# Trainium2, one core: the scan's output with tokens as rows, a fourth weight buffer, and feed-forward loops of four steps

## What is computed

```python
def step(state, inp):                      # one chunk of 32 tokens, one head, one direction
    qc, kc, vc, gc = inp
    bcum = jnp.cumsum(gc, axis=2)
    qe, ke = qc * jnp.exp(bcum), kc * jnp.exp(-bcum)
    att = jnp.where(causal_in_chunk, jnp.einsum('bhtk,bhsk->bhts', qe, ke), 0.0)
    o = jnp.einsum('bhtk,bhkv->bhtv', qe, state) + jnp.einsum('bhts,bhsv->bhtv', att, vc)
    ...
def _hg_readout(o, g, norm_w):             # o is the sum over both directions
    o = o * lax.rsqrt(jnp.mean(o * o, axis=-1, keepdims=True) + EPS)
    return o * norm_w * silu(g)
def conv_ffn_2(h, w_up, conv_w, conv_b, w_down):
    a, val = jnp.split(h @ w_up, 2, axis=-1)
    return (gelu(dwconv3(a, conv_w, conv_b)) * val) @ w_down
```

## Time and profile before

| | |
|---|---|
| median of 3 runs | 1513.62 us (1512.83 to 1514.57) |
| profiled execution, its own time | 1513.27 us |
| its span, first to last instruction | 1511.5 us |
| PE busy | 97% of the span, 10486 matmuls and as many weight loads |
| DVE busy | 72% |
| ACT busy | 48% |
| HBM read | 181 GB/s over the span |
| mean granted TensorE clock | 0.989 |

### The profile page before, as it was taken

The page is one execution under the profiler, slowest core; times in us unless marked ns, Lnnn a source line. Parts: engine busy times, 40 slices in busy tenths (PEclk is TensorE's granted clock), DMA queues, the critical chain, the costliest instruction groups (busy, mean ns, idle before and its releaser), DMA issues.

```text
span 1511.5 us, 26784 instructions
## 1 busy us (share of the span) xinstructions
PE 1461.0 (97%) x10486; PEld 1298.9 (86%) x10486; DVE 1082.4 (72%) x1659; ACT 732.3 (48%) x949; POOL 6.8 (0%) x19
## 2 busy tenths in 40 slices
PE   7989999999999999999999999899999999999997
PEld 7887889999987889999888779679999899799997
DVE  6774778778756787777766666667777768677775
ACT  6553545444545555445555433545444433454442
POOL 0000000000000000000000000000000000000000
PEclk9999999999999999999999999999999999999999
DMA  7433645555556344554526566055455554555551
GB/s 279 154 140 130 259 167 189 197 177 189 190 200 259 132 176 169 194 192 168 215 85 223 199 248 237 20 199 199 172 190 182 203 201 167 185 200 174 192 180 43
DMA packets 39677, 274.79 MB, mean 182 GB/s; under 512 B 4528, under 2 KB 5680, under 8 KB 6960
## 3 DMA queue, kind: packets, MB, share of 16 engines
q1 hardware_dynamic: 38304, 265.82, 48.9%
q0 software_dynamic: 720, 6.82, 1.2%
q10 hardware_dynamic: 576, 1.05, 0.2%
HBM read 272.62 MB, written 1.05 MB: 181 GB/s over the span
## 4 chain that ended last, share of the span: by engine, by line
PE 86%; DVE 7%; DMA 3%; ACT 3%; issue 2%; SPq 0%; DVEq 0%; ACTq 0%
PE L L1750 25%; PE D L1750 16%; PE L L1938 15%; PE L L1944 8%; PE N L1938 5%; DMA raw<-in_units 3%; PE N L1944 3%; PE M L1838 2%; DVE wlo L972 2%; PE N L1846 2%; PE D L1938 1%; PE D L2212 1%; PE N L2225 1%; DVE arena L1049 1%; PE D L1944 1%
## 5 line engine op out<-in xcount | busy, mean ns | idle before, releaser
L1750 PE MATMUL L<-h_all,whi 128*128 128x256 f32 (+1 forms) x1392 | 286.5, 305 | 14.9 <-DVE wlo L1258 7.0
L972 DVE TENSOR_TENSOR wlo<-raw,whi 128x2048 fp32r<-128x2048 f32 x106 | 242.3, 2286 | 76.9 <-ACT whi L492 76.5
L492 ACT ACTIVATE whi<-raw 128x2048 fp32r<-128x2048 f32 x106 | 202.0, 1909 | 120.7 <-PE L L1750 75.6
L1938 PE MATMUL L<-h_all,whi 128*128 128x512 f32 x992 | 252.7, 396 | 4.4 <-DVE h_all L1021 3.2
L1750 PEld LDWEIGHTS L<-h_all,whi 128*128 128x128 f32 x1392 | 228.3, 197 | 32.4 <-issue 16.4
L1134 DVE TENSOR_TENSOR wlo<-raw,whi 128x2048 fp32r<-128x2048 f32 x96 | 219.6, 2288 | 39.3 <-ACT whi L626 39.3
L1938 PEld LDWEIGHTS L<-h_all,whi 128*128 128x128 f32 x992 | 178.7, 190 | 41.4 <-DVE h_all L1021 5.1
L1750 PE MATMUL L<-h_all,wlo 128*128 128x256 f32 (+1 forms) x696 | 209.7, 301 | 0.0
L626 ACT ACTIVATE whi<-raw 128x2048 fp32r<-128x2048 f32 x96 | 182.9, 1905 | 0.0
L1750 PE MATMUL D<-hd_hi,whi 128*128 128x256 f32 x640 | 181.3, 283 | 0.0
L1750 PE MATMUL D<-hd_hi,wlo 128*128 128x256 f32 x640 | 181.1, 283 | 0.0
(11 more groups left out here) (305 smaller groups left out, 2269.0 us busy)
## 6 DMA issues: line engine op xcount, KB each, us to landing
raw<-in_units SPq DMA_DIRECT2D x250, 1024.0 KB, 4.9
arena<-in_band POOLq DMA_DIRECT2D x1, 2304.0 KB, 10.3
arena<-in_nax POOLq DMA_DIRECT2D x1, 1536.0 KB, 6.7
t<-in_mem ACTq DMA_DIRECT2D x4, 256.0 KB, 5.8
raw<-in_units SPq DMA_DIRECT2D x4, 256.0 KB, 5.4
x<-in_x SPq DMA_DIRECT2D x1, 1024.0 KB, 9.1
t<-in_ctx POOLq DMA_DIRECT2D x1, 1024.0 KB, 5.3
arena<-in_ctx POOLq DMA_DIRECT2D x1, 1024.0 KB, 7.4
```

Source lines behind the costliest of these rows:

```text
L492: A.activation(whi[weight_slot(v)][:], raw[v % RING][:], ACT.Copy).then_inc(unit_hi, 1)
L972: V.tensor_tensor(wlo[w][:], raw[v % RING][:], whi[w][:].bitcast(FP), ALU.subtract) \
L1750: ins = mm(dst, w[a], h[b], start=start and n == 0, stop=stop and n == 2, skip_group_check=True)
L1938: mm(bank[:], w[0][:, k, part * P:part * P + P], h_all[:, k, 0:512], start=k == 0, stop=False, skip_group_check=True)
```

## The change

Three edits. (1) Output of a pass: the operands change sides. The masked scores, and the 32 query columns of a chunk, are now stationary, and values and states move (128 columns); tokens are rows. A chunk's result has 32 rows, and the four chunks of a 128-token half go to the row ranges 0, 32, 64 and 96 of PSUM, each from a 32-column group of the array. The sum of squares of a token is then a sum along a row: ACT's squares (now two, of 128 columns) accumulate it, the variance is 128 x 2 elements, ACT scales the rows (two `Identity` activations), PE turns the result back (`head_turn`, two matmuls against the identity, in the odd passes and after the last), and one DVE instruction multiplies by weight and gate.

```diff
-RING = 3
+RING = 4
+SLOTS = 3
+TURN = 4
...
+            sp.dma_start(raw[3][:], io["units"][3]).then_inc(raw_full[3], 16)
...
-                with pe.Fori(2, NI - 1) as i:
-                    chunk(*looped(-1, i), i, 0)
-                    chunk(*looped(0, i), i, 1)
-                    down(1, i)
+                with pe.Fori(0, (NI - 3) // TURN) as turn:
+                    for b in range(TURN):
+                        i = turn * TURN + (2 + b)
+                        chunk(*looped(-1, b, turn), i, 0)
+                        chunk(*looped(0, b, turn), i, 1)
+                        down(*looped(1, b, turn), i)
...  (ACT's and DVE's loops in the same way)
                     A.activation(hf[1][:, h, 0:T], N0[:, 0:T], ACT.Copy).then_inc(R["hg_sq"], 1)
-                    A.activation(hf[0][:, h, 0:T], N0[:, 0:T], ACT.Square).then_inc(R["hg_sq"], 1)
+                    for tb in range(2):
+                        c = slice(tb * P, tb * P + P)
+                        A.activation(hf[0][:, h, c], N0[:, c], ACT.Square, accum_out=h_ss[:, h, tb:tb + 1]) \
+                            .then_inc(R["hg_sq"], 1)
...
-                    A.activation(rs[:], var[:], ACT.Sqrt).then_inc(R["hg_rs"], 1)
+                    A.activation(h_rs[:, h, :], h_rs[:, h, :], ACT.Sqrt).then_inc(R["hg_rs"], 1)
+                    act.wait_ge(R["hg_rs"], h + 1)
+                    for tb in range(2):
+                        c = slice(tb * P, tb * P + P)
+                        A.activation(hf[1][:, h, c], hf[1][:, h, c], ACT.Identity, scale=h_rs[:, h, tb:tb + 1]) \
+                            .then_inc(R["hg_sc"], 1)
+                if e >= 4 and e % 2 == 0:
+                    h = e // 2 - 2
                     act.wait_ge(R["hg_h"], h + 1)
                     A.activation(mix_hi[:, 4 + h, :], hf[0][:, h, T:512], ACT.Copy).then_inc(R["mix_hi_done"], 1)
...
-                    step(V.tensor_scalar(var[:], N0[:, T:512], 1.0 / P, EPS, ALU.mult, ALU.add))
+                    step(V.tensor_scalar(h_rs[:, h, :], h_ss[:, h, :], 1.0 / P, EPS, ALU.mult, ALU.add))
                     sync()
-                    V.reciprocal(var[:], var[:]).then_inc(R["hg_rv"], 1)
+                    V.reciprocal(h_rs[:, h, :], h_rs[:, h, :]).then_inc(R["hg_rv"], 1)
...
+                    dve.wait_ge(R["hg_tr"], h + 1)
+                    dve.wait_ge(R["hgq_silu"], 2 if h < 2 else 4)
+                    V.scalar_tensor_tensor(hf[0][:, h, T:512], N0[:, T:512], vc("hg_w", h), hg[:, h, :],
+                                           ALU.mult, ALU.mult).then_inc(R["hg_h"], 1)
...
+            def head_turn(h, first):
+                pe.wait_ge(R["hg_sc"], 2 * h + 2)
+                for tb in range(2):
+                    ins = mm(N0[:, T + tb * P:T + tb * P + P], hf[1][:, h, tb * P:tb * P + P], ident,
+                             start=first and tb == 0, stop=True, skip_group_check=True)
+                ins.then_inc(R["hg_tr"], 1)
...
+                if d == 1 and h:
+                    pe.wait_ge(R["hg_h"], h)
                 for tb in range(2):
-                    mm(N0[:, tb * P:tb * P + P], hv[:, tb, h * P:h * P + P], s_am[d][:, tb * P:tb * P + P],
+                    mm(N0[:, tb * P:tb * P + P], s_am[d][:, tb * P:tb * P + P], hv[:, tb, h * P:h * P + P],
                        start=d == 0 and tb == 0, stop=False, skip_group_check=True)
-                for c in range(NCH):
-                    ins = mm(N0[:, c * CH:c * CH + CH], s_st[:, c, :], s_q[d][:, c * CH:c * CH + CH],
-                             start=False, stop=d == 1 and c == NCH - 1, skip_group_check=True)
+                for tb in range(2):
+                    for c in range(4):
+                        at = (4 * tb + c) * CH
+                        ins = mm(N0[c * CH:c * CH + CH, tb * P:tb * P + P], s_q[d][:, at:at + CH], s_st[:, 4 * tb + c, :],
+                                 start=False, stop=d == 1, skip_group_check=True)
...
             job(JOBS["e_nq"][0])
-            head_sums(HGH - 1)
+            head_turn(HGH - 1, True)
...
-    nc = bacc.Bacc("TRN2", target_bir_lowering=False, num_devices=1)
+    nc = bacc.Bacc("TRN2", target_bir_lowering=False, num_devices=1, dynamic_dma_scratch_size=8192)
```

More of the change, by code:

```diff
@@ L123, in prior_job @@
 def prior_job(v):
-    return LAST[DENSE[SPLIT[v] - RING]] if SPLIT[v] >= RING else 0
+    return LAST[DENSE[SPLIT[v] - SLOTS]] if SPLIT[v] >= SLOTS else 0
 def weight_slot(v):
-    return SPLIT[v] % RING
+    return SPLIT[v] % SLOTS
 def ahead(v):
@@ L189, in build @@
         raw = [sb(f"raw{i}", [P, 2048]) for i in range(RING)]
-        whi = [sb(f"whi{i}", [P, 2048], FR) for i in range(RING)]
-        wlo = [sb(f"wlo{i}", [P, 2048], FR) for i in range(RING)]
+        whi = [sb(f"whi{i}", [P, 2048], FR) for i in range(SLOTS)]
+        wlo = [sb(f"wlo{i}", [P, 2048], FR) for i in range(SLOTS)]
         x = sb("x", [P, KB, T])
@@ L210, in build @@
         mod_mark = sb("mod_mark", [P, 1])
+        h_ss = sb("h_ss", [P, HGH, 2])
+        h_rs = sb("h_rs", [P, HGH, 2])
         mod = sb("mod", [P, 2, 48, 2])
@@ L620, in ffn, with wh @@
                 w0 = weight_slot(JOBS[name][0].unit)
[L622 to L626, removed]
+                def wh(r, b, turn):
+                    v = u0 + 3 * (2 + b) + r
+                    act.wait_ge(raw_full[v % RING], turn * (16 * 3) + 16 * (v // RING + 1))
+                    act.wait_ge(job_done, turn * (3 * TURN) + (j0 + 3 * (2 + b) + r - SLOTS + 1))
+                    A.activation(whi[(w0 + r) % SLOTS][:], raw[v % RING][:], ACT.Copy).then_inc(unit_hi, 1)
                 def low(i, r, number):
@@ L664, in ffn @@
                 hidden(1, j0 + 5)
[L665 to L674, removed]
+                with act.Fori(0, (NI - 3) // TURN) as turn:
+                    for b in range(TURN):
+                        i = turn * TURN + (2 + b)
+                        wh(1, b, turn)
+                        low(i, 0, i * 3 + (j0 - 1))
+                        low(i, 1, i * 3 + (j0 - 1))
+                        wh(2, b, turn)
+                        gate(i)
+                        low(i, 2, i * 3 + j0)
+                        low(i, 3, i * 3 + j0)
+                        wh(3, b, turn)
+                        hidden(i, i * 3 + (j0 + 2))
                 made[0] = u0 + 3 * (NI - 1) + 1
@@ L856, in _ @@
             jobs("e_hq0", lambda n, j: silu(hq[:, 0:2, :]))
-            for e in range(2 * HGH + 2):
+            for e in range(2 * HGH + 3):
                 s = e % 2
@@ L901, in _ @@
                     silu(hg[:, 2:4, :])
-                if e >= 2 and e % 2 == 0:
+                if e >= 2 and e % 2 == 0 and e <= 2 * HGH:
                     h = e // 2 - 1
@@ L1128, in ffn, with wl @@
                 at = VECS["ffn_conv"][0] + 8 * NI * f
[L1130 to L1134, removed]
+                def wl(r, b, turn):
+                    v, w = u0 + 3 * (2 + b) + r, (d0 + r) % SLOTS
+                    dve.wait_ge(unit_hi, turn * (3 * TURN) + (d0 + 3 * (2 + b) + r + 1))
+                    V.tensor_tensor(wlo[w][:], raw[v % RING][:], whi[w][:].bitcast(FP), ALU.subtract) \
+                        .then_inc(raw_used[v % RING], 1)
                 def tap(i, n):
@@ L1197, in ffn @@
                 per = 5 if scaled else 7
[L1198 to L1205, removed]
+                with dve.Fori(0, (NI - 3) // TURN) as turn:
+                    for b in range(TURN):
+                        i = turn * TURN + (2 + b)
+                        steps[0] = turn * (per * TURN) + (n0 + per * b)
+                        wl(1, b, turn)
+                        convolve(i)
+                        wl(2, b, turn)
+                        multiply(i)
+                        wl(3, b, turn)
+                        hidden(i)
                 steps[0] = n0 + per * (NI - 3)
@@ L1627, in _ @@
             passes = 2 * HGH
-            for i in range(1, passes + 3):
+            for i in range(1, passes + 4):
                 if i == passes + 1:
@@ L1635, in _ @@
                     forget(i)
[L1636 to L1645, removed]
                 if i < passes:
@@ L1651, in _ @@
                     mask(i - 1)
-                if i >= 4 and i % 2 == 0:
+                if i >= 5 and i % 2 == 1:
+                    h = (i - 5) // 2
                     dve.wait_ge(R["mix_hi_done"], MIX["B"] + h + 1)
@@ L1664, in _ @@
                         store(H_BESIDE[i - 1][0])
+                if i >= 4 and i % 2 == 0:
+                    h = i // 2 - 2
+                    dve.wait_ge(R["hg_tr"], h + 1)
+                    dve.wait_ge(R["hgq_silu"], 2 if h < 2 else 4)
+                    V.scalar_tensor_tensor(hf[0][:, h, T:512], N0[:, T:512], vc("hg_w", h), hg[:, h, :],
+                                           ALU.mult, ALU.mult).then_inc(R["hg_h"], 1)
+                if 0 < i <= passes:
                     states(i - 1)
@@ L1980, in chunk, with looped, down @@
```

(29 more changed lines are left out.)

12 lines of the change are left out of this document (5 added, 7 removed).

## The result

The changed kernel takes **1500.07 us** (median of 5 runs, 1499.74 to 1503.28) against 1513.17 us for the kernel before on the same chip. The ratio is 0.9921, 95% interval [0.9907, 0.9935]; on 1513.17 us that is -12.0 us, interval -14.1 to -9.8, and the medians differ by 13.1. The forecast was 1500.

What follows compares the result with a forecast made beforehand. PE was taken to bound the feed-forward loops and the recurrence. The edits summed to -8.4 - 5.1 + 0 = -13.5 us on 1513.27, 1499.8, with 0.35 to the median 1500.1, so 1500 us; range 1495.5 to 1508.

Steps and rivals of the forecast that it cites:

- Edit 1: Output of a recurrence pass: 10.0 us gained by overlapping column groups, less new waits; -8.4 us in sum.
- The wait in pass 6: Recurrence, pass 6: PE newly waits 0.8 us for ACT's key copy, bounds 0.3 to 1.3.
- The wait at the end: After pass 7: PE waits about 1.2 us before the last `head_turn`, bounds 0 to 3.
- `ada_row` in pass 4: Start of pass 4: PE's 0.42 us wait goes as the fourth buffer starts the transfer a unit earlier, -0.4 us.
- Edit 2: Fourth weight buffer: transfers start one unit earlier, mostly shortening band attention waits; -5.1 us, bounds 0 and -7.2.
- 3.3 of the 4.4 us: Band attention: 3.3 of PE's 4.4 us of waits for weights' low parts would go, bounds 0 and 4.4.
- rival 2: Band attention: DVE's and ACT's order is the limit, so the fourth buffer gives nothing; 1505 us, chance 0.13.
- The "half" for the clock: Behind the longest band attention wait: half of up to 1.7 us lost at 1.2 GHz is regained, 0.8 us.
- Edit 3: Longer feed-forward loops: instruction fetch at the backward branch about hidden, 0 us, bounds 0 and 8 us for PE.
- rival 1: Recurrence: ACT is late in more passes, so the gain is mostly given back; 1504 to 1506 us, chance 0.15.
- Rival 3: Output of a pass: column groups don't overlap with 32 stationary columns or this write pattern; 1510 us, chance 0.04.
- Rival 4: Feed-forward loops: backward branch refetches pages; 1508, or 1518 us and more; chance 0.08 seen, 0.05 for a slower kernel.

Runs made afterwards that it cites:

- the second comparison: The unaltered changed kernel timed again against the kernel before, on the same chip as another version: 1501.92 us, ratio 0.9934.
- one column group: Changed kernel with all sixteen output matmuls of a pass sent to the same 32 PSUM rows, output not the reference's: 1512.14 us, ratio 1.0001.
- the other chunk order: Changed kernel with the chunk loop taking both token halves of a column group before the next group: 1501.84 us, ratio 0.992.
- buffers and loops: Kernel before with four weight buffers and loops of four steps per turn, output as before: 1507.49 us, ratio 0.9963.
- the scan alone: Kernel before with only the output with tokens as rows; three weight buffers, loops of one step: 1510.07 us, ratio 0.9975.
- the loops alone: Kernel before with only loops of four steps per turn; three weight buffers, output as before: 1511.99 us, ratio 0.9994.
- eight steps a turn: Changed kernel with all eight looped feed-forward steps in one turn, no backward branch taken: 1500.73 us, ratio 0.9929.

## Why the prediction was right, step by step

**The number.** That 1500.07 us meets 1500 so closely is luck: the terms below miss by up to about 2 us each and offset each other, and the second comparison gave 1501.92. What is borne out is the mechanism and the size, -12.0 us (-14.1 to -9.8) against a forecast of -13.5.

**PE bounds, and what it loses in the recurrence the kernel wins.** Right: between 760 and 917 us the job starts move forward pass by pass, -7.5 us in all, and one column group undid all of it.

**Edit 1.** Predicted -8.4 us; the trace gives -7.5, made up so. The output: a pass with `modulate` directly behind it was (0.44 + 1.71 + 0.98) us and is (0.45 + 0.57 + 0.86), 1.25 less; where something full-width follows, 1.14 less 0.11 for the mode change, 1.03. The prediction counted seven of the first and one of the second kind. There are five and three: in passes 2 and 6 an ada row is turned first. So 5 x 1.25 + 3 x 1.03 = 9.3, not 10.0. The wait in pass 6: 0.8, as predicted. The wait at the end: 1.2, as predicted, with the low part of a weight in front of it, as described. `ada_row` in pass 4: 0.4 gained, as predicted. The last head's turn took 0.3 us more of PE than the sums, which was counted as nothing (in the chain the job starts behind it move by 1.5 us, of which 1.2 are the wait). -9.3 + 0.8 + 1.2 - 0.4 + 0.3 = -7.4. The 1.2 for the end is in part luck: the prediction's own terms, 915.1 + 0.35 - 913.9, make 1.5.

**That the edits can be priced one by one** was taken for granted, and is only half right. Priced alone, the output gives 3.8 us, not 8; its waits at the `ada_row` and at the last turn are for landings that the fourth buffer brings forward. The prediction used the fourth buffer for 0.4 us of edit 1, but the loss without it is 2.8 us of waits and two stretches at a lower clock, another 3.0.

**Edit 2.** Predicted -5.1; alone it measured -5.6 (-7.9 to -3.5). The size is right and the parts are not. The term "3.3 of the 4.4 us" of `wlo` waits was too large: 4.4 fell to 2.1 us, and the waits for the exponentials beside them (L1901) rose from 1.4 to 2.6 us in this trace and fell to 1.1 in that of the other chunk order. So both together won 1.1 us in one trace and 2.6 in the other. That is rival 2's mechanism. ACT and DVE, each in a written order, bound the band attention once landings do not; the transfers are early, the 1.85 us wait stays. The "half" for the clock did not show in this trace: a stretch at 0.51 of full over 6.9 us comes a few us later. From 396 to 508 us the nine profiles of kernels with four buffers won 1.1 to 3.3 us on the kernel before, the two with three buffers 0.3 and 0.7. The three that won least (the changed kernel's two and that of buffers and loops) have a clock of 0.97 there, the other six 0.98 and 2.2 to 3.3 us, so the clock's share comes in some executions and not in others. The wait of 1.1 us for an ada unit is gone, as predicted.

How much the buffer itself gives can be read from one pair of profiles. Up to the recurrence the changed kernel and the scan alone differ in buffers and loops only, and their clocks are nearly the same: 0.97 and 0.97 over the first 170 us, 0.86 and 0.93 from 384 to 396, 0.97 and 0.96 from 396 to 508, 1.00 in the rest. At the first scores of the recurrence the changed kernel is 4.0 us ahead (762.46 against 766.49). Of these, 2.6 us are there by the job at 158.64 us (161.23 in the scan alone), 2.0 of them one wait of the scan alone that is gone with the fourth buffer:

```profile
PE M L1857 <- DMA raw<-in_units: 2.0, 1, 2.0
```

Another 0.9 us is won between 396 and 508. In the recurrence itself buffers and loops gave 0.7 us with the old output. That makes 4.7 us at nearly equal clocks, near the prediction's 5.1, but the larger part lies in the first 160 us, where the prediction had 1.0, and not in the band attention. What the clock adds to that is left open.

**Edit 3.** Predicted 0, and 0 it is: the loops alone 0.9994, eight steps a turn the same time, 16.93 us across the branch. The rule of the Trainium skill in "Runtime: NRT & Kernel Launch", section "Instruction fetch mechanics", by which a taken branch to a page outside the window of two held pages must wait for its transfer, would have acted here, as the target lies 58 KB, some 3.5 packets, back. The trace does not agree: there is no hole, and no page of instructions came twice. The larger instruction memory that the same section gives PE fits what was measured. The page of the profile counts the packets: 58, 69 and 83 packets with one, four and eight steps a turn. Three more copies of a step in each of four layers are 12 x 14.5 KB, or 11 packets of 16 KB; seven are 28 x 14.5 KB, or 25. Each page came once, so the 58 KB turn was still held when the branch went back. What the loops do for the kernel is another thing: a step takes three units, so with four buffers the pattern of buffers repeats only after four steps. The fourth buffer needs them.

**Rivals.** The recurrence's gain given back (rival 1) is what happened without the fourth buffer, 1510.07 us, by waits for landings and not by ACT's longer path. Rival 3 is what one column group does: 1512.14 us against the 1510 worked out. The prediction called itself wrong if the chain of passes 5 to 7 ran through ACT; it does so only for the 3.7 us before pass 6's updates, which is one of the two waits that it had counted. Rival 4 is ruled out by the packets; its 1518 us was too low for its own condition, as 32 us more than the forecast would be 1532.

## What to carry to other kernels

When a change makes the bounding engine faster in one stage, look at once at the landing times behind it: here 9 us of PE work saved was worth 4 us with three weight buffers and 6 to 7.5 with four. Small float32 matmuls with a 32-column stationary side paid here only because they went to different column groups; then four cost little more than one. Before putting a short scaling between an output and a matmul, look at what long weight work stands in front of it in each engine's written order, and put the matmul one job later.

## What the runs showed of the chip that was not expected

- Four column groups overlapped in full in float32 even with 32-column stationary operands that change with each matmul: sixteen in 0.57 us, in one group 1.75 us for fifteen. Their order made no difference.
- A float32 matmul with 32 stationary and 128 moving columns takes about as long as one with 128 and 32: (1.75 - 0.11) / 15 = 0.109 us, with the 0.11 for the change of mode taken off, against 0.107.
- Going from full-width to column-group matmuls or back costs 0.11 us each time, at every such place of the recurrence. The Trainium skill, "TensorEngine Tiling (Array Packing)", section "Key Properties", says that a change of the tiling mode drains the engine and gives no price; the trace agrees, with this number.
- The place where the clock falls changes from one profile to the next. Over the first 170 us the granted clock was 0.97 in the profiles of the kernel before and of the changed one, 0.99 in three of the experiments, and the job at 159.70 us started 1.1 us earlier in the one of the changed kernel above, 0.6 us later in its second profile, and 1.9 to 3.8 us earlier in those three. Long loops with three buffers are among the three, and they timed as before. So a difference of two profiles is read stage by stage here, and not from their ends.
